# Scan rows in four DRAM copies, fetched per tile by four transfers of 32 partitions

## The reference, cut to what matters

```python
a_cs = jnp.cumsum(dt * a_head.reshape(SSD_G, e), axis=2)
seg = a_cs[:, :, :, None] - a_cs[:, :, None, :]
decay = jnp.exp(jnp.where(lower, seg, -jnp.inf))
...
y_diag = jnp.einsum('bclsge,bcsgep->bclgep', cb[..., None] * decay, xdt)
...
y_off = jnp.einsum('bclgn,bcgepn,bclge->bclgep', cmat, s_in, jnp.exp(a_cs))
```

## Time and profile before

| | |
|---|---|
| timed runs, median (three) | 1156.92 us |
| profiled execution | 1160.04 us |
| its span, first to last instruction | 1158.2 us |
| mean granted TensorE clock | 0.963 |
| PE busy | 1065.1 us (92%) |
| DVE busy | 674.9 us (58%) |
| ACT busy | 644.0 us (56%) |
| POOL busy | 312.5 us (27%) |
| row fetches `rowb<-acs_rows` | 48, 256 KB each, median 5.2 us to landing |

### The profile page before, as it was taken

The page is one execution under the profiler, slowest core; times in us unless marked ns, Lnnn a source line. Parts: engine busy times, 40 slices in busy tenths (PEclk is TensorE's granted clock), DMA queues, the critical chain, the costliest instruction groups (busy, mean ns, idle before and its releaser), DMA issues.

```text
span 1158.2 us, 16832 instructions
## 1 busy us (share of the span) xinstructions
PE 1065.1 (92%) x5726; PEld 835.6 (72%) x5726; DVE 674.9 (58%) x1124; ACT 644.0 (56%) x1155; POOL 312.5 (27%) x265
## 2 busy tenths in 40 slices
PE   5899998899899999999799999978878989999997
PEld 1785654446857888887499999957767976778885
DVE  1432663434355999996565640177766134798994
ACT  2523432445245887886555452398775424588880
POOL 0520920003202000001436655655556600100000
PEclk9899999999988999999899999998898999899999
DMA  9643527993139999995323333476630304999973
GB/s 385 237 182 145 200 109 284 423 420 132 64 114 358 411 411 411 411 409 199 140 73 113 110 111 143 148 214 188 189 119 1 145 1 161 378 412 410 411 311 128
DMA packets 86368, 266.71 MB, mean 230 GB/s; under 512 B 7329, under 2 KB 39585, under 8 KB 73249
## 3 DMA queue, kind: packets, MB, share of 16 engines
q1 hardware_dynamic: 78496, 243.30, 55.6%
q0 software_dynamic: 2880, 12.58, 2.9%
q10 hardware_dynamic: 4928, 10.01, 2.4%
HBM read 245.68 MB, written 15.47 MB: 225 GB/s over the span
## 4 chain that ended last, share of the span: by engine, by line
PE 71%; ACT 8%; DMA 8%; DVE 7%; POOL 3%; issue 2%; SPq 0%; ACTq 0%; POOLq 0%; DVEq 0%
PE bank L2117 16%; PE bank L2118 16%; PE bank L2119 16%; PE bank L2141 3%; PE bank L2401 3%; POOL wlo L736 2%; PE bank L2203 2%; ACT seg L1349 2%; PE bank L2659 2%; DMA h_blk<-h_rows,tok_of 2%; DMA modb<-modb 1%; PE bank L2376 1%; ACT whi L883 1%; DMA rowb<-acs_rows 1%; DMA modw<-wide_mods 1%
## 5 line engine op out<-in xcount | busy, mean ns | idle before, releaser
L736 POOL TENSOR_TENSOR wlo<-raw,whi 128x512 fp32r<-128x512 f32 x152 | 201.0, 1356 | 264.7 <-ACT whi L883 258.9
L2117 PE MATMUL bank<-hhi,whi 128*128 128x384 f32 (+1 forms) x504 | 176.9, 351 | 12.9 <-DVE hlo L1471 9.5
L2118 PE MATMUL bank<-hlo,whi 128*128 128x384 f32 (+1 forms) x504 | 173.3, 344 | 0.0
L2119 PE MATMUL bank<-hhi,wlo 128*128 128x384 f32 (+1 forms) x504 | 173.0, 343 | 0.0
L1849 DVE TENSOR_TENSOR wlo<-raw_more,whi 128x1024 fp32r<-128x1024 f32 x108 | 128.7, 1222 | 14.4 <-ACT whi L1146 12.9
L1849 DVE TENSOR_TENSOR wlo<-raw,whi 128x1024 fp32r<-128x1024 f32 x108 | 128.2, 1221 | 10.3 <-ACT whi L1146 8.1
L1146 ACT CAST whi<-raw_more 128x1024 fp32r<-128x1024 f32 x108 | 111.5, 1049 | 29.6 <-PE bank L2119 25.4
L1146 ACT CAST whi<-raw 128x1024 fp32r<-128x1024 f32 x108 | 111.5, 1053 | 22.6 <-PE bank L2119 12.3
L2117 PE MATMUL bank<-whi,blk_hi 128*128 128x512 f32 x288 | 115.1, 400 | 0.0
L2118 PE MATMUL bank<-wlo,blk_hi 128*128 128x512 f32 x288 | 113.8, 395 | 0.0
L2119 PE MATMUL bank<-whi,blk_lo 128*128 128x512 f32 x288 | 113.7, 395 | 0.0
(11 more groups left out here) (355 smaller groups left out, 1996.6 us busy)
## 6 DMA issues: line engine op xcount, KB each, us to landing
raw<-stream SPq DMA_DIRECT2D x56, 1024.0 KB, 4.8
raw<-experts SPq DMA_DIRECT2D x108, 512.0 KB, 11.4
raw_more<-experts SPq DMA_DIRECT2D x108, 512.0 KB, 11.3
modw<-wide_mods SPq DMA_DIRECT2D x37, 1024.0 KB, 12.5
rowb<-acs_rows SPq DMA_DIRECT2D x48, 256.0 KB, 5.2
shared<-shared SPq DMA_DIRECT2D x6, 1024.0 KB, 6.1
h_next<-h_blk SPq DMA_DIRECT2D x9, 512.0 KB, 10.6
y_rows<-y_sb ACTq DMA_DIRECT2D x9, 512.0 KB, 6.7
```

Source lines behind the costliest of these rows:

```text
L736: ins = pool.tensor_tensor(wlo[:, q % SPL, w], raw[:, pos % RAW, w], whi[:, q % SPL, w].bitcast(F32), ALU.subtract)
L2117: pe.matmul(dst, whi_, xhi_, start=first, stop=False)
L2118: pe.matmul(dst, whi_, xlo_, start=False, stop=False)
L2119: return pe.matmul(dst, wlo_, xhi_, start=False, stop=last)
```

## The change

`acs_rows` becomes a tensor of four copies, each laid out tile by tile: [4, 3, 64, 128], so that the four rows of one direction and tile are 2 KB in one piece. ACT writes it with four DMAs in place of one, each of 64 x 3 pieces of 512 B. `fetch_rows(n)` issues four DMAs in place of two: the one of copy c writes the 32 partitions from 32 c on, both directions together, in pieces of 2 KB (128 KB each). The bytes of a fetch stay the same, 512 KB a step. The waits count four transfers in place of one (`acs_out`) and of two (`rowb_in`).

```diff
+ROW_COPIES = 4
...
-        acs_dram = nc.dram_tensor("acs_rows", [64, NTOK], F32).ap()
+        acs_dram = nc.dram_tensor("acs_rows", [ROW_COPIES, TILES, 64, P], F32).ap()
...
                 hg, t = n // TILES, n % TILES
-                for dr in range(2):
-                    r = dr * 32 + 4 * hg
-                    sp.dma_start(rowb[:, n % ROWS, dr, :].rearrange("p (h l) -> p h l", h=4),
-                                 acs_dram[r:r + 4, t * P:(t + 1) * P].partition_broadcast(P)).then_inc(
+                share = P // ROW_COPIES
+                for c in range(ROW_COPIES):
+                    rows = acs_dram[c, t].rearrange("(d g) l -> d g l", d=2)[:, 4 * hg:4 * hg + 4, :]
+                    sp.dma_start(rowb[share * c:share * (c + 1), n % ROWS, :, :],
+                                 rows.rearrange("d h l -> d (h l)").partition_broadcast(share)).then_inc(
                         rowb_in[n % ROWS], 16)
...
-            sp.wait_ge(acs_out, 16)
+            sp.wait_ge(acs_out, 16 * ROW_COPIES)
...
-            act.dma_start(acs_dram, acsT[0:64, :]).then_inc(acs_out, 16)
+            for c in range(ROW_COPIES):
+                act.dma_start(acs_dram[c].rearrange("t r l -> r t l"),
+                              acsT[0:64, :].rearrange("r (t l) -> r t l", t=TILES)).then_inc(acs_out, 16)
...
-                dve.wait_ge(rowb_in[n % ROWS], 32 * (n // ROWS + 1))
+                dve.wait_ge(rowb_in[n % ROWS], 16 * ROW_COPIES * (n // ROWS + 1))
```

## The result

The changed kernel takes 1165.24 us (median of 19 runs, 1160.95 to 1168.79), the kernel before, timed beside it, 1160.30 us (19 runs, 1156.52 to 1164.21). That is within the 1% that was called no change, but the time lies 3.2 us above the range of the prediction. About 3.4 us of the 8.2 us between forecast and measurement are the base: the median of the first three runs, 1156.92, lay at the low end of the 19.

What follows compares the result with a forecast made beforehand. PE held 71% of the span, but in the scan no engine was full: PE, DVE and ACT waited in a ring. Scan -1.5 us and write +1.5 us summed to 0 on 1156.92: forecast 1157 us, range 1153 to 1162.

Steps and rivals of the forecast that it cites:

- applying the difference to the median: Base of the whole forecast: the profiled 1160.04 us was 3.1 us above the median, so the median 1156.92 was used.
- With three dimensions on both sides, as these have, I take 0.5: +1.5 us (1.1 to 1.6).: Write in the projections: three more DMA issues on ACT at 0.5 us each delay the split of `xsw1`, +1.5 us.
- I cost it at nothing: Projections after the write: TensorE's clock falling after PE's longer wait, priced at nothing, with 2 us kept for the range.
- Rival 4: PE's gap at 622 us brings TensorE's clock down, costing 2 us: 1159; chance 6%.
- Together -1.5 us: Scan: rows landing 1.0 us sooner give back 0.9 us at step 19 and 0.6 us at step 23.
- The clean landing: Row fetch in the scan: last byte 4.5 us after the first issue in place of 5.5, 1.0 us a step sooner.
- 256 KB in 1.4 us is 187 GB/s.: Row fetch at step 5: rate read from the distance of two landings, leaving about 2.7 us fixed and 2 x 1.4 data.
- The upper end: Row fetch: 128 KB take 0.4 us at 347 GB/s, so the last of four transfers lands at 4.3 us.
- Rival 1: Scan fetch is no faster: 1158.4 us, or 1160.3 up to 1162 with the landing 0.7 us later; chance 27%.
- waits grow and new ones come: Scan, landing 0.7 us later: some 6 us more DVE time waiting for rows, 1.8 us more on the path: 1160.3.
- Rival 2: Scan: the whole DVE wait for rows, up to 5.1 us, comes back: 1153.3 us, or 1152; chance 17%.
- Rival 3: Scan fetch: four transfers take a full turn of 1.4 us each, landing 2.8 us later: 1178 us; chance 5%.

Runs made afterwards that it cites:

- e1: Kernel before plus three further copies written by ACT at the same place that nobody reads, fetch untouched; ratio 1.0029 to the kernel before.
- e2: Changed kernel with one copy written once in the new layout, all four parts of the fetch reading it; ratio 1.0018 to the kernel before.
- e18: Same kernel as e2, timed a second time; ratio 1.0009 to the kernel before.
- e4: One copy in the new layout, fetched by two transfers of 128 partitions in 2 KB pieces, no split; ratio 1.0007 to the kernel before.
- e3: Changed kernel with the first copy written where it was and the other three later, in the z projections; ratio 1.0052 to the kernel before.
- e11: Same kernel as e3, timed a second time; ratio 1.0023 to the kernel before.
- e17: Copies written late as in e3, but all four parts of a fetch read copy 0; ratio 1.0015 to the kernel before.
- e9: Kernel before with five row buffers in place of four, each fetch one step earlier; ratio 1.0001 to the kernel before.
- e16: e4 (one copy, new layout, no split) with five row buffers; 1157.82 us, ratio 0.9969 to the kernel before.
- e5: Changed kernel with the first two weight pieces of the scan loaded at its start; ratio 1.0049 to the kernel before.
- e13: Changed kernel with the scan's second weight piece loaded after step 17 in place of 16; ratio 1.0044 to the kernel before.

## Why the prediction was wrong

1. **The base.** The forecast stands on 1156.92 us; 19 runs gave 1160.30. That is 3.4 us of the error, and no reasoning about the change could mend it; that the profiled execution took 1160.04 was a hint that I set aside by "applying the difference to the median".
2. **"With three dimensions on both sides, as these have, I take 0.5: +1.5 us (1.1 to 1.6)."** This term was mis-sized, and its bounds with it: I had priced a write to DRAM by reads from it, and by a simpler pattern. The four took 2.83 us, +2.3. That PE's gap came out at 2.38 us, not far from the forecast 2.0, is luck: ACT's wait of 0.75 us for DVE lay behind the write, the prediction did not count it, and it took up part of the delay. The path was right: ACT, the split of `xsw1`, POOL's low part, PE, and behind PE's gap nothing gave the time back.
3. **"I cost it at nothing"**, of TensorE's clock. Rival 4 happened in the profile: granted clock 0.50 at 628 to 630 us, 1.2 to 1.6 us more in the stage. Against it I had set a wait of 1.6 us that left the clock at 1.00; e1 shows that even 2.65 us can. A chance near one half, not 6%, is what the four profiles give.
4. **"Together -1.5 us"**, of the scan. This step failed. The clean landing was forecast well (4.5 us, measured 4.7), and then I carried this 1.0 us over to steps 19 and 23. At step 23 the wait did go, from 1.7 to 0.34 us. Step 19 is not clean: its rows stand behind a 1 MB piece. There the last part landed after 11.5 us, not 7.7, and the wait went from 1.61 to 6.47 us. I had treated a step's rows as one transfer: they are there when the last of four is, and read from four copies under load the parts spread (6.3 to 11.5 us in step 19; 7.0 to 7.7 from one copy, e2). Timed alone, the split showed a loss of 1 to 2 us (e2, e18) in place of the gain of 1.5, which lies outside both intervals; no change at all lies inside.
5. **"256 KB in 1.4 us is 187 GB/s."** The trace of before does not bear this reading out. Between the two landings of step 5 (771.5 and 772.9 us) the engines moved little, some 46 KB (columns as in the earlier trace rows):

```profile
771.50:772.00 0.50, 0.50 (x9) 0.33 (x6) 0.50 (x2) 0.50 (x2) 0.00 (x0) 1.00 0.13 40
772.00:772.50 0.50, 0.50 (x3) 0.45 (x3) 0.50 (x2) 0.50 (x2) 0.14 (x1) 1.00 0.12 37
772.50:773.00 0.50, 0.50 (x4) 0.42 (x4) 0.50 (x2) 0.30 (x1) 0.50 (x1) 1.00 0.05 15
```

   The window of 768 to 770 us did not hold this fetch alone either: the two transfers of step 4 landed in it, at 768.3 and 769.4. So the division into 2.7 us fixed and 2 x 1.4 us of data is not shown, and it is luck that 4.5 us came near 4.7. (The two issues were read in the wrong order as well: the first took 0.36 us, the second 0.51, which changes no sum.) The upper end needed 2 KB pieces to go faster. Of rates, the page shows only this: the queue moved the same 243.30 MB in 60832 packets instead of 78496, and its share of the engines' time went from 55.6% to 55.5%. Fewer, larger pieces used no less of them.
6. **The rivals.** Rival 1 had nearly the right price for its case (with the real base 1161.8 to 1163.7, at its upper end 1165.4) and the right sign, by the wrong mechanism: the parts do land sooner where nothing else runs. Its second half, "waits grow and new ones come", did happen, but e1 shows as much waiting with the old fetch. By the rule of the Trainium skill, "DMA: Bandwidth & Descriptors", section "Rules for kernel authors", that the sum was weighed against, splitting gains nothing. The runs agree in that (1.0018 and 1.0009 split, 1.0007 unsplit). Rival 2 is refuted by e4, where most of the DVE wait did come back and the time did not move. Rival 3 did not occur: no step took a full turn per part.

**The sum as measured:** 1.8 to 3.4 us for the write in the profiles (3.4 timed in e1), 1 to 2 us for the split, together 2.8 to 5.4, against 4.8. Of the two only the write is clear of noise. And the sum does not close from the other side: with the writes moved out of the way e3 and e11 should have come down to the split's price and took 6.0 and 2.7 us. Reading four different copies at 2 to 3 us would fill that, but with it the changed kernel's sum is 4.8 to 8.4 us, of which only the lower end fits. By the medians, where e3 and e11 are 3.7 and 2.4 us slower, less is missing. **Open**, then, is what the reading of four copies costs and why, to some 2 us. Copies read by an unsplit fetch were not tried.

## What to carry to other kernels

Price an added DMA issue by the same engine, direction and number of dimensions, and see who waits for that engine's next instruction; a stretch where the engine stands idle hides them, as the stage showed in e3, e11 and e17, though the total did not show the gain. A transfer in parts is as late as its latest part: judge it at the steps behind bulk loads, not at clean ones. A fetch can be made faster (e4), or given a buffer more (e9), without any gain; here both together gained 3.6 us (e16). A base for a difference of 0.4% needs more than three runs.

## What the runs showed of the hardware

- A DMA from 64 partitions to DRAM took ACT 0.51 us to issue with two dimensions (e1) and 0.58 to 0.78 us with three (e3, changed kernel), once 1.22 (e1).
- A PE gap of 2.2 to 2.7 us in a dense stretch was followed by a granted clock of 0.50 in two profiles of four (2.38 us in the changed kernel, 2.34 in e5) and not in the other two (2.65 in e1, 2.24 in e13), with the same code around it. In the 16 profiles with one or two writes the clock stayed at 1.00 through that stage.
- Under a 1 MB load on the same queue, four parts issued within 1.7 us landed 6.3 to 11.5 us after their issue when they read four copies (changed kernel) and 7.0 to 7.7 when they read one (e2); in a clean step 3.1 to 3.4 us (changed kernel).
- Between the two landings of one fetch, 1.4 us apart, the DMA engines moved 15 to 40 GB/s (before, step 5): the distance of two landings of 256 KB was no rate.
- Fewer packets for the same bytes (60832 for 78496) left the queue's share of the engines' time where it was (55.5%, 55.6%).
